# Two feed-forwards on one core: the high and low part of h side by side in one 512-column product

## The chip, the cores and the metric

The kernel runs on one core of one Trainium2 chip, in one launch. The metric is the device time of one execution in microseconds. TensorE multiplies matrices, VectorE and ScalarE do elementwise work, GpSimd a little of it, and SyncE issues most of the transfers.

## The reference, cut to what matters

The whole program is a small model of 256 tokens with width 1024: two blocks with attention mixers and a feed-forward each, then a block with a delta-rule mixer and a layer of product-key experts. Only the two feed-forwards (layers 0 and 1) are touched:

```python
h = rms_norm(x, ffn_norm[i]) * (1.0 + sc_f) + sh_f
x = x + g_f * swiglu(h, ffn_w_gate[i], ffn_w_up[i], ffn_w_down[i])
```

Here `swiglu` is `(silu(h @ w_gate) * (h @ w_up)) @ w_down`, with 2816 hidden columns. All is float32.

## The kernel before

A float32 value is held as a high part, rounded to the format that TensorE multiplies in one pass (fp32r), and a low part, the remainder. A product of two such values is three products: high by high, low by high and high by low. The fourth is left out.

A feed-forward is one stage, `swiglu` (L1625). The 2816 hidden columns are cut into 22 tiles of 128. For tile i the weights are u (gate and up columns, 1 MB, halves 0 and 1 of 1024 columns) and v (down rows, 0.5 MB). The normed and modulated h lies turned, as `h_hi` and `h_lo`, each 128 x 8 x 256. The work of tile i:

- SyncE loads u, v and a chunk of the modulation weights of the next layer (1 MB), on one queue, u and v three tiles ahead.
- ScalarE casts u to its high part (`high_u`, L1773), VectorE subtracts to get the low part (`low_u`, L1809); v the same way (L1779, L1814).
- TensorE, `up(i)`: for each half and each of 8 chunks of the inner dimension three products with 256 columns (the tokens), L1728 to L1730, summed in PSUM tile `pa`. The first tile is in `up_first` (L1713 to L1715), interleaved with the transposes of the norm (L544).
- ScalarE takes Silu of the gate half (L1798), VectorE multiplies it by the up half (L1838), rounds (L1842) and subtracts (L1844): the coefficients `c_hi` and `c_lo`.
- TensorE, `down(i)`: 12 products with 512 columns (L1742, L1743, L1746), summed over all tiles in `py`.

TensorE's order is `up_first`, two products that sum a gate row over the partitions (`Sums`, L221; layer 0 only), and then `up(i)`, `down(i-1)` for i from 1 to 21, and `down(21)`. ScalarE's order per tile is Silu(i), cast of u for tile i+2, cast of v for tile i+1. VectorE's is multiply, round, subtract, low part of u for i+2, low part of v for i+1, and then the modulation's folds: `Modulation.fold` (L200) multiplies a chunk of weights by a column and adds it to a row, 128 x 2048. `fold_at` spreads the folds over tiles 2 to 20; one tile has none, one or two. Layer 0 folds each of 20 chunks into one row. Layer 1 folds its first 8 chunks into two rows and 12 into one. Each engine runs its own list in order; between engines there are semaphores, and each buffer of u_hi, u_lo, v_hi, v_lo, c_hi, c_lo, pa and act_out exists twice. After the last tile the sum in `py` is scaled and added to x (L1860, L1862).

Of the kernel before, what the change touches and what calls it, by code (L numbers as in the profile page):

```python
# [1624 lines left out]
def swiglu(nc, name, k, feeds, h_split, x, ahead, gate, ada, row, feeds_ahead):  # L1625
# [4 lines left out]
    h_hi, h_lo = h_split  # L1630
    first = ada[2]
    chunks = ada[3] - first
    with Stage(nc, name) as st:
        sums = Sums(nc, k, st, row, (10, 11), 2) if row is not None else None
        u_hi, u_lo = (st.sb(n, [P, 2, 2 * D], F32R) for n in ("u_hi", "u_lo"))
        v_hi, v_lo = (st.sb(n, [P, 2, D], F32R) for n in ("v_hi", "v_lo"))
        act_out = st.sb("act_out", [P, 2, S])
        coef = st.sb("coef", [P, S])
        c_hi, c_lo = (st.sb(n, [P, 2, S], F32R) for n in ("c_hi", "c_lo"))
        pa = st.ps("pa", [P, 2, CW])  # L1640
        py = st.ps("py", [P, TT * 2, CW])
# [15 lines left out]
        pcols = pa[:, tiles % 2, 0:2 * KT]  # L1657
# [40 lines left out]
        def _(pe):  # L1698
            def up_first():
# [4 lines left out]
                for c in range(KT):  # L1704
# [3 lines left out]
                    for half in range(2):  # L1708
                        if c % 4 == 0:
                            pe.wait_ge(u_split_first, c // 2 + half + 1)  # L1710
                        out = pa[:, 0, half * S:(half + 1) * S]
                        cols = slice(half * D + c * P, half * D + (c + 1) * P)
                        pe.matmul(out, u_hi[:, 0, cols], h_hi[:, c, :], start=(c == 0 and half == 0), stop=False)  # L1713
                        pe.matmul(out, u_hi[:, 0, cols], h_lo[:, c, :], start=False, stop=False)
                        last = pe.matmul(out, u_lo[:, 0, cols], h_hi[:, c, :], start=False,  # L1715
                                         stop=(c == KT - 1 and half == 1))
# [40 lines left out]
            pe.wait_ge(weighed, tiles - 1)  # L1757
# [48 lines left out]
        def _(dve):  # L1806
# [26 lines left out]
            for i in range(tiles):  # L1833
                b = i % 2
                dve.wait_ge(acted, i + 1)
                if i >= 1:
# [1960 lines left out]
```

## Time and profile before

| | |
|---|---|
| time, median of 3 runs | 2159.97 us (2158.83 to 2162.43) |
| the profiled execution | 2154.51 us, span 2152.7 us |
| granted TensorE clock, mean | 0.955 |
| TensorE busy (matmuls) | 1963.3 us, 91% of the span |
| VectorE busy | 1616.8 us, 75% |
| ScalarE busy | 982.0 us, 46% |
| tiles of layer 0's feed-forward | about 253 to 450 us of the span |
| tiles of layer 1's feed-forward | about 624 to 827 us of the span |

The profile is of one execution. Matmuls are pipelined, so the record of one lasts until its results are out and overlaps the next; their spacing is read from starts. A granted clock of 1.00 is 2.4 GHz, 0.50 is 1.2 GHz. An arrow in a row names the instruction that ended the idle time ahead of it. Starts are microseconds from the start of the span.

### The profile page before, as it was taken

What the parts mean: (1) busy time and instruction counts of PE and PEld (TensorE: products, weight loads), DVE (VectorE), ACT (ScalarE), POOL (GpSimd) and SP (SyncE); (2) the same over time, 40 slices, a digit from 0 to 9 for tenths busy, and PEclk for the clock granted to TensorE, in tenths of its full rate; (3) what the DMA queues carried; (4) which work ended last, traced back from release to release, by engine and by line L of the source; (5) the groups of instructions that cost most, each with busy time, mean ns of one, the idle gap of its engine ahead of it and who ended that gap; (6) DMA issues with size and microseconds to landing.
All of it is one profiled execution on the core that took longest, in us unless ns stands there. A gap on an engine that the chain in (4) does not pass through costs nothing. (4 is left out here: it accounts for less than half of the span.)

```text
span 2152.7 us, 40884 instructions
## 1 busy us (share of the span) xinstructions
PE 1963.3 (91%) x16381; PEld 1775.2 (82%) x16381; DVE 1616.8 (75%) x2682; ACT 982.0 (46%) x1758; POOL 437.4 (20%) x238
## 2 busy tenths in 40 slices
PE   8967899989779998998788888999999999999997
PEld 4954899988579997878787878999999998888886
DVE  3757787857658996776566574599999997877786
ACT  2527434336554333324344544454455554445553
POOL 1000000000230001431000300478677770000000
PEclk9979999989889998997899989999999999999999
DMA  7771698825148792312200034466566666777775
GB/s 251 254 201 60 229 341 310 287 108 193 64 147 292 284 342 89 103 55 81 79 4 4 2 138 157 154 219 206 188 196 200 199 205 216 243 243 240 241 243 192
DMA packets 184769, 390.65 MB, mean 181 GB/s; under 512 B 14922, under 2 KB 130298, under 8 KB 173050
## 3 DMA queue, kind: packets, MB, share of 16 engines
q1 hardware_dynamic: 166050, 371.21, 51.5%
q10 hardware_dynamic: 18530, 16.82, 2.3%
q8 instruction: 131, 2.15, 0.4%
q14 instruction: 58, 0.48, 0.1%
HBM read 368.58 MB, written 19.40 MB: 180 GB/s over the span
## 5 line engine op out<-in xcount | busy, mean ns | idle before, releaser
L3443 POOL TENSOR_TENSOR peer_lo<-peer_u,peer_hi 128x1024 fp32r<-128x1024 f32 x117 | 299.1, 2561 | 108.4 <-ACT peer_hi L3573 108.3
L3620 PE MATMUL route_pa<-all_h_hi,peer_hi 128*128 128x256 f32 x1024 | 291.6, 285 | 8.3 <-POOL peer_lo L3443 6.5
L3621 PE MATMUL route_pa<-all_h_lo,peer_hi 128*128 128x256 f32 x1024 | 290.7, 284 | 0.0
L3622 PE MATMUL route_pa<-all_h_hi,peer_lo 128*128 128x256 f32 x1024 | 290.5, 284 | 0.0
L1466 ACT CAST peer_hi<-peer_u 128x1024 fp32r<-128x1024 f32 x126 | 132.8, 1054 | 174.4 <-PE experts_py L1449 170.2
L3620 PEld LDWEIGHTS route_pa<-all_h_hi,peer_hi 128*128 128x128 f32 x1024 | 197.3, 193 | 9.9 <-POOL peer_lo L3443 7.9
L1445 PE MATMUL experts_py<-peer_hi,experts_c_hi 128*128 128x512 f32 x512 | 200.3, 391 | 3.6 <-DVE experts_c_lo L1506 3.6
L1446 PE MATMUL experts_py<-peer_lo,experts_c_hi 128*128 128x512 f32 x512 | 200.2, 391 | 0.0
L3621 PEld LDWEIGHTS route_pa<-all_h_lo,peer_hi 128*128 128x128 f32 x1024 | 197.3, 193 | 0.0
L3622 PEld LDWEIGHTS route_pa<-all_h_hi,peer_lo 128*128 128x128 f32 x1024 | 197.2, 193 | 0.0
L1728 PE MATMUL ffn_pa<-all_h_hi,ffn_u_hi 128*128 128x256 f32 x672 | 191.2, 285 | 3.0 <-DVE ffn_u_lo L1809 3.0
L1730 PE MATMUL ffn_pa<-all_h_hi,ffn_u_lo 128*128 128x256 f32 x672 | 191.2, 285 | 0.0
L1729 PE MATMUL ffn_pa<-all_h_lo,ffn_u_hi 128*128 128x256 f32 x672 | 191.1, 284 | 0.0
L1449 PE MATMUL experts_py<-peer_hi,experts_c_lo 128*128 128x512 f32 x512 | 158.2, 390 | 0.0
L1500 DVE TENSOR_TENSOR peer_lo<-peer_u,peer_hi 128x1024 fp32r<-128x1024 f32 x126 | 153.5, 1219 | 0.0
L3579 ACT ACTIVATE peer_g<-route_pa 128x256 f32<-128x256 f32 x128 | 49.1, 383 | 195.4 <-PE route_pa L3622 195.4
L3573 ACT CAST peer_hi<-peer_u 128x1024 fp32r<-128x1024 f32 x127 | 133.6, 1052 | 2.7 <-DMA peer_u<-in_peer_u 2.5
L1728 PEld LDWEIGHTS ffn_pa<-all_h_hi,ffn_u_hi 128*128 128x128 f32 x672 | 129.8, 193 | 5.6 <-DVE ffn_u_lo L1809 4.0
L1729 PEld LDWEIGHTS ffn_pa<-all_h_lo,ffn_u_hi 128*128 128x128 f32 x672 | 129.8, 193 | 1.5
L1730 PEld LDWEIGHTS ffn_pa<-all_h_hi,ffn_u_lo 128*128 128x128 f32 x672 | 129.8, 193 | 0.0
L876 PE MATMUL proj_psum<-proj_w_hi,all_h_hi 128*128 128x256 f32 (+1 forms) x384 | 112.2, 292 | 13.0 <-DVE proj_w_lo L912 13.0
L1445 PEld LDWEIGHTS experts_py<-peer_hi,experts_c_hi 128*128 128x128 f32 x512 | 96.4, 188 | 24.3 <-DVE experts_c_lo L1506 3.1
(608 smaller groups left out, 5313.8 us busy)
## 6 DMA issues: line engine op xcount, KB each, us to landing
peer_u<-in_peer_v SPq DMA_DIRECT2D x128, 512.0 KB, 3.8
peer_u<-in_peer_u SPq DMA_DIRECT2D x125, 512.0 KB, 3.6
l_w<-in_ffn_columns SPq DMA_DIRECT2D x44, 1024.0 KB, 8.8
ffn_ada_w<-in_ada_w SPq DMA_DIRECT2D x40, 1024.0 KB, 6.1
ffnw_v<-in_ffn_rows SPq DMA_DIRECT2D x44, 512.0 KB, 4.8
hid_kept<-peer_g ACTq DMA_DIRECT2D x128, 128.0 KB, 1.7
all_main<-hid_kept SPq DMA_DIRECT2D x128, 128.0 KB, 3.7
l_w<-in_diff_w_in SPq DMA_DIRECT2D x12, 1024.0 KB, 5.5
```

Source lines behind the costliest of these rows:

```text
L1445: pe.matmul(py[:, 2 * t + n, :], c_hi[:, b, part], v_hi[:, r, cols], start=start, stop=False)
L1446: pe.matmul(py[:, 2 * t + n, :], c_hi[:, b, part], v_lo[:, r, cols], start=False, stop=False)
L1449: last = pe.matmul(py[:, 2 * t + n, :], c_lo[:, b, part], v_hi[:, r, cols], start=False, stop=stop)
L1500: dve.tensor_tensor(v_lo[:, r, :], feed_v.slot(i), v_hi[:, r, :].bitcast(F32), ALU.subtract).then_inc(v_split, 1)
L1728: pe.matmul(out, u_hi[:, b, cols], h_hi[:, c, :], start=(c == 0), stop=False)
L1729: pe.matmul(out, u_hi[:, b, cols], h_lo[:, c, :], start=False, stop=False)
L1730: last = pe.matmul(out, u_lo[:, b, cols], h_hi[:, c, :], start=False, stop=(c == KT - 1))
L3443: pool.tensor_tensor(u_lo[:, i % ring, :], raw_u(i), u_hi[:, i % ring, :].bitcast(F32), ALU.subtract).then_inc(u_split, 1)
L3573: act.copy(u_hi[:, i % ring, cols], raw_u(i)[:, cols]).then_inc(u_hi_ready, 1)
L3620: pe.matmul(out, u_hi[:, b, cols], h_hi[:, c, :], start=(c == 0), stop=False)
L3621: pe.matmul(out, u_hi[:, b, cols], h_lo[:, c, :], start=False, stop=False)
L3622: last = pe.matmul(out, u_lo[:, b, cols], h_hi[:, c, :], start=False, stop=(c == KT - 1))
```

## The change

`h_hi` and `h_lo` become the two halves of one tile `h_pair`, so that for a chunk their columns lie side by side. The high part of a weight is then multiplied by both with one product of 512 columns, whose two halves of 256 are different sums; the low part of the weight is multiplied by `h_hi` into the first half. `pa` grows to four banks (two tiles by gate and up). ScalarE copies the second halves (gate and up, 2 x 256) out of PSUM to `second`, and VectorE adds them to the first halves: first the gate's, then the up's. Silu then runs on the sum in SBUF. The summing of the gate row uses `pa`'s second half as its PSUM and stands ahead of `up_first`; `up(1)` waits until its results are copied out.

```diff
-    def __init__(self, nc, k, st, row, jobs, banks):
+    def __init__(self, nc, k, st, row, jobs, banks, psum=None):
-        self.psum = st.ps("sum_psum", [P, banks, CW])
+        self.psum = st.ps("sum_psum", [P, banks, CW]) if psum is None else psum
...
-        act_out = st.sb("act_out", [P, 2, S])
-        coef = st.sb("coef", [P, S])
+        gate_sum, up_sum = (st.sb(n, [P, 2, S]) for n in ("gate_sum", "up_sum"))
-        pa = st.ps("pa", [P, 2, CW])
+        pa = st.ps("pa", [P, 2, 2, CW])
+        sums = Sums(nc, k, st, row, (10, 11), 2, pa[:, 1]) if row is not None else None
...
+        second = full[:, 0:2, :]
...
+            def row_products(pe, b, half, c):
+                cols = slice(half * D + c * P, half * D + (c + 1) * P)
+                pe.matmul(pa[:, b, half, :], u_hi[:, b, cols], h_pair[:, c].rearrange("p a s -> p (a s)"),
+                          start=(c == 0), stop=False)
+                return pe.matmul(pa[:, b, half, 0:S], u_lo[:, b, cols], h_hi[:, c, :], start=False, stop=(c == KT - 1))
...
             def up(i):
...
                 if i >= 2:
-                    pe.wait_ge(weighed, i - 1)
+                    pe.wait_ge(up_summed, i - 1)
+                elif sums:
+                    pe.wait_ge(sums.moved, len(sums.jobs))
                 for half in range(2):
-                    out = pa[:, b, half * S:(half + 1) * S]
                     for c in range(KT):
-                        cols = slice(half * D + c * P, half * D + (c + 1) * P)
-                        pe.matmul(out, u_hi[:, b, cols], h_hi[:, c, :], start=(c == 0), stop=False)
-                        pe.matmul(out, u_hi[:, b, cols], h_lo[:, c, :], start=False, stop=False)
-                        last = pe.matmul(out, u_lo[:, b, cols], h_hi[:, c, :], start=False, stop=(c == KT - 1))
+                        last = row_products(pe, b, half, c)
...
-            up_first()
             if sums:
                 sums.sum(pe)
+            up_first()
...
                 act.wait_ge(rows_ready, i + 1)
-                if i >= 2:
-                    act.wait_ge(weighed, i - 1)
-                act.activation(act_out[:, i % 2, :], pa[:, i % 2, 0:S], ACT.Silu).then_inc(acted, 1)
+                if i:
+                    act.wait_ge(up_summed, i)
+                act.copy(second, pa[:, i % 2, :, S:2 * S]).then_inc(second_ready, 1)
+                act.wait_ge(gate_summed, i + 1)
+                act.activation(gate_sum[:, i % 2, :], gate_sum[:, i % 2, :], ACT.Silu).then_inc(acted, 1)
...
+                dve.wait_ge(second_ready, i + 1)
+                if i >= 2:
+                    dve.wait_ge(coef_ready, i - 1)
+                for half, (to, done) in enumerate(((gate_sum, gate_summed), (up_sum, up_summed))):
+                    dve.tensor_tensor(to[:, b, :], pa[:, b, half, 0:S], second[:, half, :], ALU.add).then_inc(done, 1)
+                dve.wait_ge(up_summed, i + 1)
                 dve.wait_ge(acted, i + 1)
-                if i >= 1:
-                    dve.wait_ge(coef_ready, i)
-                dve.tensor_tensor(coef[:], act_out[:, b, :], pa[:, b, S:2 * S], ALU.mult).then_inc(weighed, 1)
+                dve.tensor_tensor(up_sum[:, b, :], gate_sum[:, b, :], up_sum[:, b, :], ALU.mult).then_inc(weighed, 1)
...
-                dve.tensor_copy(c_hi[:, b, :], coef[:]).then_inc(rounded, 1)
+                dve.tensor_copy(c_hi[:, b, :], up_sum[:, b, :]).then_inc(rounded, 1)
...
-        h_hi, h_lo = (pst.sb(n, [P, KT, S], F32R) for n in ("h_hi", "h_lo"))
-        k["h_hi"], k["h_lo"] = h_hi, h_lo
+        k["h_pair"] = pst.sb("h_pair", [P, KT, 2, S], F32R)
+        k["h_hi"], k["h_lo"] = (k["h_pair"][:, :, i, :] for i in range(2))
```

## Rows read from the trace of the kernel before

**Rows 1.** The page's first part: busy time, share of the span, instructions.

```profile
PE 1963.3 (91%) x16381; PEld 1775.2 (82%) x16381; DVE 1616.8 (75%) x2682; ACT 982.0 (46%) x1758; POOL 437.4 (20%) x238
```

**Rows 2.** Busy time by stretch, tiles of layer 0 and 1; clock, DMA share and GB/s last.

```profile
267.00:447.00 180.00, 180.00 (x1264) 169.32 (x1263) 139.83 (x127) 68.07 (x65) 0.67 (x1) 1.00 0.84 295
647.00:825.00 178.00, 177.75 (x1251) 167.16 (x1250) 155.36 (x135) 63.81 (x61) 0.00 (x0) 1.00 0.78 281
```

**Rows 3.** TensorE's timeline in one tile of layer 0: start, us, instruction.

```profile
299.80 0.28 PE L1728 MATMUL ffn_pa<-all_h_hi,ffn_u_hi 128*128 128x256 f32 x1
...
305.56 0.40 PE L1742 MATMUL ffn_py<-ffn_v_hi,ffn_c_hi 128*128 128x512 f32 x1
...
308.30 0.28 PE L1728 MATMUL ffn_pa<-all_h_hi,ffn_u_hi 128*128 128x256 f32 x1
```

**Rows 4.** Groups of instructions, 645 to 825 us (layer 1): busy, mean ns, idle before.

```profile
L200 DVE SCALAR_TENSOR_TENSOR all_main<-ffn_ada_w,all_main 128x2048 f32<-128x2048 f32 x28 | 65.4, 2347 | 0.5
...
L1809 DVE TENSOR_TENSOR ffn_u_lo<-l_w,ffn_u_hi 128x2048 fp32r<-128x2048 f32 x19 | 43.5, 2288 | 6.1 <-ACT ffn_u_hi L1773 6.1
...
L1838 DVE TENSOR_TENSOR ffn_coef<-ffn_act_out,ffn_pa 128x256 f32<-128x256 f32 x21 | 8.8, 418 | 10.5 <-ACT ffn_act_out L1798 10.5
```

**Rows 5.** ScalarE and VectorE, timeline of one tile of layer 0.

```profile
305.75 0.38 ACT L1798 ACTIVATE ffn_act_out<-ffn_pa 128x256 f32<-128x256 f32 x1 [4.64 <-PE ffn_pa L1730]
...
306.04 1.91 ACT L1773 CAST ffn_u_hi<-l_w 128x2048 fp32r<-128x2048 f32 x1
306.17 0.42 DVE L1838 TENSOR_TENSOR ffn_coef<-ffn_act_out,ffn_pa 128x256 f32<-128x256 f32 x1 [0.95 <-ACT ffn_act_out L1798]
...
306.63 0.29 DVE L1842 CAST ffn_c_hi<-ffn_coef 128x256 fp32r<-128x256 f32 x1
...
306.96 0.42 DVE L1844 TENSOR_TENSOR ffn_c_lo<-ffn_coef,ffn_c_hi 128x256 fp32r<-128x256 f32 x1
...
307.98 2.29 DVE L1809 TENSOR_TENSOR ffn_u_lo<-l_w,ffn_u_hi 128x2048 fp32r<-128x2048 f32 x1 [0.60 <-ACT ffn_u_hi L1773]
...
310.19 1.22 DVE L1814 TENSOR_TENSOR ffn_v_lo<-ffnw_v,ffn_v_hi 128x1024 fp32r<-128x1024 f32 x1
...
311.32 2.35 DVE L200 SCALAR_TENSOR_TENSOR all_main<-ffn_ada_w,all_main 128x2048 f32<-128x2048 f32 x1
```

**Rows 6.** VectorE's timeline in layer 1: two folds in one tile, and the multiply behind.

```profile
676.92 4.80 DVE L200 SCALAR_TENSOR_TENSOR all_main<-ffn_ada_w,all_main 128x2048 f32<-128x2048 f32 x2
681.64 0.41 DVE L1838 TENSOR_TENSOR ffn_coef<-ffn_act_out,ffn_pa 128x256 f32<-128x256 f32 x1
...
693.92 4.61 DVE L200 SCALAR_TENSOR_TENSOR all_main<-ffn_ada_w,all_main 128x2048 f32<-128x2048 f32 x2
698.45 0.41 DVE L1838 TENSOR_TENSOR ffn_coef<-ffn_act_out,ffn_pa 128x256 f32<-128x256 f32 x1
```

**Rows 7.** Groups of ScalarE: the copy of 128x512 out of PSUM.

```profile
L227 ACT COPY all_main<-ffn_sum_psum 128x512 f32<-128x512 f32 x2 | 1.2, 585 | 0.3 <-PE ffn_sum_psum L221 0.3
```

**Rows 8.** Both stages' heads: timeline of TensorE, second Silu, and busy time by stretch.

```profile
250.95 1.86 PE L544 MATMUL ffn_py<-ffn_norm_diag,all_main 128*128 128x128 f32 x7 [3.41 <-DVE ffn_norm_diag L568]
...
263.19 1.88 PE L221 MATMUL ffn_sum_psum<-all_main,all_ones 128*128 128x512 f32 x4
265.70 0.39 PE L1728 MATMUL ffn_pa<-all_h_hi,ffn_u_hi 128*128 128x256 f32 x1 [0.63 <-DVE ffn_u_lo L1809]
...
271.75 0.39 ACT L1798 ACTIVATE ffn_act_out<-ffn_pa 128x256 f32<-128x256 f32 x1 [1.62 <-PE ffn_pa L1730]
...
638.30 0.39 PE L1728 MATMUL ffn_pa<-all_h_hi,ffn_u_hi 128*128 128x256 f32 x1 [2.35 <-DVE ffn_u_lo L1809]
...
645.86 0.38 ACT L1798 ACTIVATE ffn_act_out<-ffn_pa 128x256 f32<-128x256 f32 x1 [4.56 <-PE ffn_pa L1730]
...
250.00:256.00 6.00, 5.05 (x23) 5.02 (x24) 4.75 (x13) 3.10 (x6) 0.00 (x0) 0.50 0.56 225
638.00:642.00 4.00, 3.70 (x18) 3.71 (x19) 3.93 (x6) 3.28 (x4) 4.00 (x3) 0.59 0.38 121
```

More of the change, by code:

```diff
@@ L1630, in swiglu @@
     h_hi, h_lo = h_split
+    h_pair = k["h_pair"]
     first = ada[2]
@@ L1633, in swiglu @@
     with Stage(nc, name) as st:
-        sums = Sums(nc, k, st, row, (10, 11), 2) if row is not None else None
         u_hi, u_lo = (st.sb(n, [P, 2, 2 * D], F32R) for n in ("u_hi", "u_lo"))
         v_hi, v_lo = (st.sb(n, [P, 2, D], F32R) for n in ("v_hi", "v_lo"))
-        act_out = st.sb("act_out", [P, 2, S])
-        coef = st.sb("coef", [P, S])
+        gate_sum, up_sum = (st.sb(n, [P, 2, S]) for n in ("gate_sum", "up_sum"))
         c_hi, c_lo = (st.sb(n, [P, 2, S], F32R) for n in ("c_hi", "c_lo"))
-        pa = st.ps("pa", [P, 2, CW])
+        pa = st.ps("pa", [P, 2, 2, CW])
         py = st.ps("py", [P, TT * 2, CW])
-        u_hi_ready, u_split, v_hi_ready, v_split, rows_ready, acted, weighed, rounded, coef_ready, down_done, \
+        sums = Sums(nc, k, st, row, (10, 11), 2, pa[:, 1]) if row is not None else None
+        u_hi_ready, u_split, v_hi_ready, v_split, rows_ready, second_ready, gate_summed, up_summed, acted, weighed, rounded, coef_ready, down_done, \
             scaled, summed = (st.sem(n) for n in (
-                "u_hi_ready", "u_split", "v_hi_ready", "v_split", "rows_ready", "acted", "weighed", "rounded",
-                "coef_ready", "down_done", "scaled", "added"))
+                "u_hi_ready", "u_split", "v_hi_ready", "v_split", "rows_ready", "second_ready", "gate_summed",
+                "up_summed", "acted", "weighed", "rounded", "coef_ready", "down_done", "scaled", "added"))
         beside = Modulation(nc, k, st, *ada)
@@ L1656, in swiglu @@
         columns = Columns(st, k, "ahead", *ahead, k["cols"])
-        pcols = pa[:, tiles % 2, 0:2 * KT]
+        pcols = pa[:, tiles % 2, 0, 0:2 * KT]
         tmp = feed_v.slot(0).rearrange("p (a n) -> p a n", a=2)
@@ L1710, in up_first @@
                             pe.wait_ge(u_split_first, c // 2 + half + 1)
-                        out = pa[:, 0, half * S:(half + 1) * S]
-                        cols = slice(half * D + c * P, half * D + (c + 1) * P)
[L1713 to L1716, printed above, removed]
+                        last = row_products(pe, 0, half, c)
                 last.then_inc(rows_ready, 1)
@@ L1722, in up @@
                 if i >= 2:
-                    pe.wait_ge(weighed, i - 1)
+                    pe.wait_ge(up_summed, i - 1)
+                elif sums:
+                    pe.wait_ge(sums.moved, len(sums.jobs))
                 for half in range(2):
-                    out = pa[:, b, half * S:(half + 1) * S]
                     for c in range(KT):
-                        cols = slice(half * D + c * P, half * D + (c + 1) * P)
-                        pe.matmul(out, u_hi[:, b, cols], h_hi[:, c, :], start=(c == 0), stop=False)
-                        pe.matmul(out, u_hi[:, b, cols], h_lo[:, c, :], start=False, stop=False)
-                        last = pe.matmul(out, u_lo[:, b, cols], h_hi[:, c, :], start=False, stop=(c == KT - 1))
+                        last = row_products(pe, b, half, c)
                 last.then_inc(rows_ready, 1)
@@ L1756, in _ @@
             down(tiles - 1)
-            pe.wait_ge(weighed, tiles - 1)
+            pe.wait_ge(up_summed, tiles - 1)
             pe.wait_ge(beside.folded, chunks)
@@ L1841, in _ @@
                     dve.wait_ge(down_done, i - 1)
-                dve.tensor_copy(c_hi[:, b, :], coef[:]).then_inc(rounded, 1)
+                dve.tensor_copy(c_hi[:, b, :], up_sum[:, b, :]).then_inc(rounded, 1)
                 dve.wait_ge(rounded, i + 1)
-                dve.tensor_tensor(c_lo[:, b, :], coef[:], c_hi[:, b, :].bitcast(F32), ALU.subtract
+                dve.tensor_tensor(c_lo[:, b, :], up_sum[:, b, :], c_hi[:, b, :].bitcast(F32), ALU.subtract
                                   ).then_inc(coef_ready, 1)
```

## The prediction, made before the change was timed

> **What bounds the kernel now.** I read the page's first part, then the busy time by stretch, then the timeline inside one feed-forward tile, because the change touches nothing outside the two feed-forward stages. Over the whole span TensorE is busy 91% and VectorE 75% [rows 1], but both are averages over many stages. In the two stretches that hold nearly all of the feed-forward tiles TensorE is busy 180.00 of 180.00 us and 177.75 of 178.00 us at a granted clock of 1.00, VectorE 139.83 of 180.00 in layer 0 and 155.36 of 178.00 in layer 1 [rows 2]. So TensorE bounds both stages, and in layer 1 VectorE is only 13% behind it.
>
> Matmul records overlap, so their durations (0.28 us for 256 columns, 0.40 us for 512, [rows 3]) are no price; the distance between starts is. In one tile of layer 0 the 48 products with 256 columns take 299.80 to 305.56, 5.76 us or 120.0 ns each; the 12 products with 512 columns take 305.56 to 308.30, 2.74 us or 228.3 ns each [rows 3]. The two together are a tile: 8.50 us.
>
> VectorE's tile comes from starts in the same way [rows 5]: gate multiply 306.17, rounding 306.63, remainder 306.96, then nothing until 307.98, because the low part of u waits for ScalarE's cast of u (306.04 + 1.91 = 307.95); low part of u 2.21 us to the next start, low part of v 1.13 us, then the modulation folds. Two folds in a row take 4.72 us (676.92 to 681.64) or 4.53 us (693.92 to 698.45) [rows 6]; I take 2.31 us for one. Layer 0 has 20 folds for tiles 2 to 20. Layer 1 has 28, because its first 8 chunks are folded into two rows [rows 4].
>
> **TensorE's part.** Each (chunk, half) had three 256-column products, 3 x 120.0 = 360 ns; it now has one of 512 and one of 256, 228.3 + 120.0 = 348 ns. The columns streamed are the same 768. 16 pairs per tile save 0.19 us: a tile of 8.31 us. For 21 tiles of a stage after the first that is 3.9 us. In the first tile the products run between the norm's transposes, and its 16 pairs save 0.2 us. The trace has no 512 followed by a 256 with other weights; the bounds are 0 (360 ns) and 40 ns (768 columns at the 2.4 GHz that a granted clock of 1.00 is, 320 ns). I take 12, by the rows of the same stage.
>
> The row on this first: 120.0 ns for 256 columns and 228.3 for 512 leave about 13 to 15 ns per matmul above the columns' own time. The Trainium skill, TensorE: Matmul & The Clock Gate, section Back-to-back issue gap, gives for isolated matmuls columns / 2.4 GHz plus about 2.5 ns; by that rule one matmul less would be worth 2.5 ns, not 12. The trace does not agree with it in size, so the rows decide; what a small saving would do is a rival below.
>
> **VectorE's part.** Added per tile: two additions of 128x256, one operand in PSUM. The nearest row is today's gate multiply with the same shape and operands, 418 ns [rows 4]. The multiply, now all in SBUF, I leave at its price. Removed: nothing. The additions are 0.84 us per tile of busy time.
>
> **ScalarE's part.** Added: one copy of 128x512 out of PSUM, 585 ns [rows 7]. ScalarE is busy 68.07 of 180.00 us [rows 2], so the copy itself is covered. It costs through its place: Silu and the cast of u stand behind it and behind the new wait for VectorE's gate sum. Today, when VectorE is late, ScalarE has run ahead, its cast is done, and VectorE does not wait: over all of layer 1 the low part of u waited only 6.1 us for it [rows 4], though one wait is 0.60 us [rows 5] and there are 20 tiles. After the change Silu(i) needs the gate sum of tile i, and the cast of u for tile i+2 is queued behind Silu(i). So VectorE waits for that cast in every tile, however late it is itself.
>
> VectorE's tile from the start of the gate addition, all steps from [rows 5]: addition 0.42, to ScalarE 0.04 (305.75 + 0.38 to 306.17, the other way round), Silu's start to cast's start 0.29 (305.75 to 306.04), cast and handover 1.94. The low part of u starts at 2.69. Inside this lie the second addition, the multiply (from 0.88), rounding (1.34) and remainder (1.67, done at 2.09): they leave VectorE idle for 0.6. Then 2.21 + 1.13: folds start at 6.03.
>
> *Layer 0:* tiles 2 to 20 take 19 x 6.03 + 20 x 2.31 = 160.8 us, less 2.9 in tile 20, which has no u left to split (its low part of v starts at 2.0 and not at 4.90): 157.9. TensorE needs 19 x 8.31 = 157.9. A tie: TensorE keeps its gain, with no reserve. At the end the last coefficient comes at 0.82 (handover, copy 0.59, handover) + 2.14 = 2.96 us after the last u product, while the down product of the tile before covers 2.74: 0.2 us exposed. Sum: -3.9 - 0.2 + 0.2 = -3.9.
>
> *Layer 1:* 19 x 6.03 + 28 x 2.31 - 2.9 = 176.4 us. TensorE needs 157.9. **VectorE becomes the bound.** Buffers let it lag some 5 us, but this lag is not forgiven at the end, since the last down product needs the last coefficient. From the end of tile 2's u products to the end of the last down product: 0.82 + 176.4 + 2.14 + 2.74 = 182.1. Today: 19 x 8.50 + 2 x 2.74 = 167.0. So +15.1, less 0.6 that the tiles 0 to 2 save on TensorE: +14.5.
>
> **The moved sums (layer 0 only).** Two products of the gate row stood between the first tile and the second at 263.19 [rows 8], taking 1.9 us in time in which TensorE would have waited for the low part of u anyway: it still idled 0.63 us until 265.70 [rows 8]. They now run at the stage's start, before the transposes, where TensorE is idle for 3.41 us until 250.95 [rows 8]. They come ahead of the transposes on the queue; at full clock they are covered, at half clock (3.8 us) they delay them by about 0.7. ScalarE's moves of their results (two of 585 ns, [rows 7]) stand behind the first cast of v and end before 265.7, so the second tile waits for nothing new. Two sides through the clock: today the head, 250 to 256, runs at a granted 0.50, which is 1.2 GHz, after that idle stretch [rows 8]. 5.05 us were busy there; if the sums keep the clock up, at most 2.5 come back; I take 2.0. The gap they filled is left empty, as it is in layer 1 today: 2.35 us idle before 638.30, and then 0.59 granted in 638 to 642 [rows 8]. From the second tile's first product to its Silu it takes 7.56 us there (638.30 to 645.86), against 6.05 in layer 0 (265.70 to 271.75) [rows 8]: 1.5 lost. Net -0.5, with bounds -2.0 and +2.2.
>
> The one layout change, h_hi and h_lo as halves of one tile, leaves each slice contiguous; I cost it at nothing for every other stage.
>
> **Sum.** -3.9 (layer 0) + 14.5 (layer 1) - 0.5 (sums) = +10.1 us. The profiled execution took 2154.51 us (span 2152.7), so the same execution would give 2164.6; the median of the three runs is 5.5 higher, 2159.97, and from it I get **2170 us**, 0.5% slower.
>
> **The rivals.** What the measurement can tell from no change is 0.2%, 4.3 us.
> 1. *VectorE keeps TensorE's pace in layer 1* (the other side). It decides from a VectorE tile of 8.31 us, that is 4.9 without the folds' 3.4 (28 x 2.31 / 19), where I have 6.03. Then both layers keep TensorE's gain: twice -4.1 (21 x 0.19 and 0.2 at the head) less 0.2 each at the end, -0.5 for the sums: -8.3, 2152. For it: VectorE idles 22.6 us in layer 1 now [rows 2], more than 19 x 0.84 = 16 us of additions. Against it: the wait for the cast must vanish and the additions shrink by half. Chance 0.09.
> 2. *Only the wait for the cast vanishes.* VectorE's steps back to back are 0.34 + 0.46 + 0.46 + 0.33 + 0.34 + 2.21 + 1.13 = 5.27 us; layer 1 then takes 19 x 0.76 - 0.8 = 13.7 us less than forecast (in tile 20 nothing waited for a cast): -3.6, 2156 to 2160 with the bounds, mostly within 0.2%. Against it: the program order on ScalarE. Chance 0.09. That matmul records mean what they say (3 x 0.28 against 0.40 + 0.28 us, 704 pairs, 113 us less) is excluded by the starts 120 ns apart.
> 3. *The smaller saving.* With 0 to 3 ns per pair layer 0 gains nothing and layer 1 does not change: +14.5, 2174. By the rule cited above it would be 352 x 2.5 ns = 0.9 us in layer 0, 2173. Chance 0.2, inside the forecast's range.
> 4. *The clock falls in the waits of layer 1.* TensorE would idle about 1 us per tile, up to 2.3 in one piece behind two folds, as long as the gap before 638.30. Each fall costs about 1.5 us, but the idle time takes it in while VectorE is the bound. 0 to +4: 2174. Chance 0.12.
> The forecast with rivals 3 and 4: 0.82.
>
> **How the numbers follow.** Layer 1 between +12 (folds at 2.26, quicker handovers) and +19 (clock, slower ones); layer 0 between -4.5, VectorE's tie, and +0.5; sums -2.0 to +2.2. Likely together +2.5 to +18.5: 2162.5 to 2178.5. That leaves out rivals 1 and 2 and little else, under 0.2.
>
> **What would show it.** Right: in layer 1 starts of Silu (now every 8.50 us) 9.3 apart on average, TensorE waiting there some 15 us for coefficients or the low part of u; VectorE's low part of u waiting about 0.6 us for ScalarE's cast in nearly each tile of both layers; in layer 0 a period of 8.31 and the 512-column product followed 228 ns later. Wrong: TensorE still busy all of layer 1's stretch; additions under 0.3 us; pairs at 360 ns or 330; a VectorE that starts the low part of u right behind the remainder.

## The result, and the profile after

The changed kernel takes 2172.33 us (median of 9 runs, 2167.78 to 2177.0) against 2159.97 (9 runs, 2155.27 to 2165.2): a ratio of 1.0059 (1.0044 to 1.0075), 0.6% slower. The forecast was 2170, range 2162.5 to 2178.5.

The page's first part, of the changed kernel, answers to [rows 1]:

```profile
span 2171.5 us, 39659 instructions
...
PE 1968.2 (91%) x15677; PEld 1740.3 (80%) x15677; DVE 1648.2 (76%) x2770; ACT 1006.1 (46%) x1802; POOL 437.5 (20%) x238
```

704 matmuls fewer, 88 VectorE and 44 ScalarE instructions more. The span of this one execution is 18.8 us longer than that of the one before, where the medians differ by 12.4. Of the 18.8, 14.8 lie in the two stages, and the rest, 1.4 ahead of them and 2.6 behind, in code that did not change.

Each stage begins with ScalarE's Square (L549), so the distance to the next stage's Square is the stage's time. Instructions of line L549, kernel before; the last two numbers of a row are the first and last start:

```profile
L549 ACT ACTIVATE ffn_full<-all_main x2: 1057/1057/1057, 248.1 to 621.2; 128x1024 f32<-128x1024 f32 x2
...
L549 ACT ACTIVATE proj_full<-all_main x1: 1057/1057/1057, 453.1 to 453.1; 128x1024 f32<-128x1024 f32 x1
...
L549 ACT ACTIVATE dnb_h_t<-all_main x1: 1057/1057/1057, 827.2 to 827.2; 128x1024 f32<-128x1024 f32 x1
```

The same of the changed kernel:

```profile
L549 ACT ACTIVATE ffn_full<-all_main x2: 1057/1057/1057, 249.5 to 621.5; 128x1024 f32<-128x1024 f32 x2
...
L549 ACT ACTIVATE proj_full<-all_main x1: 1057/1057/1057, 453.5 to 453.5; 128x1024 f32<-128x1024 f32 x1
...
L549 ACT ACTIVATE dnb_h_t<-all_main x1: 1057/1057/1057, 843.3 to 843.3; 128x1024 f32<-128x1024 f32 x1
```

Layer 0: 205.0 before, 204.0 after, -1.0. Layer 1: 206.0 before, 221.8 after, **+15.8**. Between the two stages, all of the loss is in layer 1. These two differences are of one execution of each kernel; runs below whose code in a stage is the same as here differ there by 1.3 us (layer 1) and 2.1 us (layer 0).

What the span gained behind the two stages is in large part one place, 32 products of one column each (L509) in the delta-rule mixer. TensorE's timeline, kernel before and changed kernel:

```profile
1259.98 3.77 PE L509 MATMUL dnon_pcols<-all_ones,all_main 128*128 128x1 f32 x32
...
1276.32 6.83 PE L509 MATMUL dnon_pcols<-all_ones,all_main 128*128 128x1 f32 x32
```

The granted clock is 1.00 in the first (1260.0 to 1263.0 us) and 0.50 in the second (1276.3 to 1279.3): 3.1 us for the same instructions. In the profiles of all eleven kernels with the new feed-forward (this one and e1 to e3, e5 to e11) they take 6.8 us, in those of the kernel before and e4 3.8. So this seems to come with the change, though by what path no run shows.

Busy time by stretch of the changed kernel (the first two answer to [rows 2], the last two to the heads in [rows 8]; clock, DMA share and GB/s last):

```profile
267.00:447.00 180.00, 179.84 (x931) 152.91 (x931) 154.62 (x170) 78.80 (x86) 0.30 (x1) 0.99 0.84 295
647.00:825.00 178.00, 168.33 (x848) 140.64 (x847) 159.78 (x160) 69.96 (x77) 0.00 (x0) 0.97 0.79 277
...
250.00:256.00 6.00, 4.59 (x25) 3.20 (x24) 4.86 (x14) 4.44 (x11) 0.00 (x0) 1.00 0.74 264
266.00:272.00 6.00, 6.00 (x22) 5.13 (x21) 5.20 (x8) 3.81 (x4) 1.30 (x1) 0.55 0.64 199
```

TensorE still fills layer 0 and no longer fills layer 1, where it idles 9.7 of 178 us. VectorE's groups in layer 1 (645 to 840 us; busy, mean ns, idle before) answer to [rows 4]:

```profile
L200 DVE SCALAR_TENSOR_TENSOR all_main<-ffn_ada_w,all_main 128x2048 f32<-128x2048 f32 x28 | 65.4, 2346 | 0.5
L1811 DVE TENSOR_TENSOR ffn_u_lo<-l_w,ffn_u_hi 128x2048 fp32r<-128x2048 f32 x20 | 45.8, 2292 | 9.8 <-ACT ffn_u_hi L1773 9.8
...
L1844 DVE TENSOR_TENSOR ffn_up_sum<-ffn_gate_sum,ffn_up_sum 128x256 f32<-128x256 f32 x21 | 8.9, 426 | 4.7 <-ACT ffn_gate_sum L1800 4.7
...
L1841 DVE TENSOR_TENSOR ffn_gate_sum<-ffn_pa,ffn_full 128x256 f32<-128x256 f32 x21 | 8.8, 417 | 2.7 <-ACT ffn_full L1798 2.7
L1841 DVE TENSOR_TENSOR ffn_up_sum<-ffn_pa,ffn_full 128x256 f32<-128x256 f32 x21 | 8.7, 414 | 0.0
```

The additions cost 415 ns each, as priced. VectorE waits for its input (L1841) only 2.7 us in 21 tiles: it is the bound. TensorE in turn waits for VectorE's coefficients:

```profile
PE ffn_py L1742 <- DVE ffn_c_lo L1850: 10.5, 8, 2.1
```

(From `--waits`, 640 to 838 us: us in total, times, longest.) The prediction had some 15 us here. And yet VectorE waits 9.8 + 4.7 us for ScalarE inside its own chain. One tile of layer 0 in VectorE's timeline shows how, beside [rows 5]:

```profile
318.70 0.42 DVE L1841 TENSOR_TENSOR ffn_gate_sum<-ffn_pa,ffn_full 128x256 f32<-128x256 f32 x1
319.03 0.41 DVE L1841 TENSOR_TENSOR ffn_up_sum<-ffn_pa,ffn_full 128x256 f32<-128x256 f32 x1
319.67 0.43 DVE L1844 TENSOR_TENSOR ffn_up_sum<-ffn_gate_sum,ffn_up_sum 128x256 f32<-128x256 f32 x1 [0.23 <-ACT ffn_gate_sum L1800]
...
321.40 2.29 DVE L1811 TENSOR_TENSOR ffn_u_lo<-l_w,ffn_u_hi 128x2048 fp32r<-128x2048 f32 x1 [0.52 <-ACT ffn_u_hi L1773]
...
324.75 2.35 DVE L200 SCALAR_TENSOR_TENSOR all_main<-ffn_ada_w,all_main 128x2048 f32<-128x2048 f32 x1
327.01 0.42 DVE L1841 TENSOR_TENSOR ffn_gate_sum<-ffn_pa,ffn_full 128x256 f32<-128x256 f32 x1
```

The low part of u starts 2.70 us behind the gate addition (forecast 2.69), the fold 6.05 (forecast 6.03), the next tile 8.31. In layer 1 the gate additions of tiles 2 and 21 start at 655.53 and 831.86, 176.3 us apart (9.28 us a tile); the forecast was 176.4.

TensorE's timeline in a tile of layer 0 of the changed kernel, against [rows 3]:

```profile
302.75 0.40 PE L1702 MATMUL ffn_pa<-all_h_pair,ffn_u_hi 128*128 128x512 f32 x1
302.98 0.28 PE L1704 MATMUL ffn_pa<-all_h_pair,ffn_u_lo 128*128 128x256 f32 x1
303.09 0.40 PE L1702 MATMUL ffn_pa<-all_h_pair,ffn_u_hi 128*128 128x512 f32 x1
303.33 0.28 PE L1704 MATMUL ffn_pa<-all_h_pair,ffn_u_lo 128*128 128x256 f32 x1
303.44 0.40 PE L1702 MATMUL ffn_pa<-all_h_pair,ffn_u_hi 128*128 128x512 f32 x1
```

Over the 16 pairs from 301.69 to 307.33 a pair takes 352.5 ns: 239 behind the wide product and 114 behind the narrow one. It saves 7.5 ns, not 12, and TensorE's tile is 8.385 us, not 8.31.

### The profile page after: what moved, and what is told of

The parts are those of the page before. It is cut to its first block and busy times, and to the rows that moved or that the text cites. A ratio compares the mean times of both kernels' runs of the same rounds, so it can differ in the third digit from the quotient of the medians.

```text
span 2171.5 us, 39659 instructions
## 1 busy us (share of the span) xinstructions
PE 1968.2 (91%) x15677; PEld 1740.3 (80%) x15677; DVE 1648.2 (76%) x2770; ACT 1006.1 (46%) x1802; POOL 437.5 (20%) x238
## 5 line engine op out<-in xcount | busy, mean ns | idle before, releaser
L3626 PE MATMUL route_pa<-all_h_pair,peer_hi 128*128 128x256 f32 x1024 | 291.9, 285 | 7.5 <-POOL peer_lo L3449 5.7
L3627 PE MATMUL route_pa<-all_h_pair,peer_hi 128*128 128x256 f32 x1024 | 291.1, 284 | 0.0
L3628 PE MATMUL route_pa<-all_h_pair,peer_lo 128*128 128x256 f32 x1024 | 291.0, 284 | 0.0
L1702 PE MATMUL ffn_pa<-all_h_pair,ffn_u_hi 128*128 128x512 f32 x704 | 257.0, 406 | 5.4 <-DVE ffn_u_lo L1811 4.7
L3626 PEld LDWEIGHTS route_pa<-all_h_pair,peer_hi 128*128 128x128 f32 x1024 | 197.8, 193 | 9.0 <-POOL peer_lo L3449 6.9
L1704 PE MATMUL ffn_pa<-all_h_pair,ffn_u_lo 128*128 128x256 f32 x704 | 199.6, 284 | 0.0
L3628 PEld LDWEIGHTS route_pa<-all_h_pair,peer_lo 128*128 128x128 f32 x1024 | 197.8, 193 | 0.0
L3627 PEld LDWEIGHTS route_pa<-all_h_pair,peer_hi 128*128 128x128 f32 x1024 | 197.8, 193 | 0.0
L1702 PEld LDWEIGHTS ffn_pa<-all_h_pair,ffn_u_hi 128*128 128x128 f32 x704 | 135.0, 192 | 40.0 <-DVE ffn_u_lo L1811 6.3
L1704 PEld LDWEIGHTS ffn_pa<-all_h_pair,ffn_u_lo 128*128 128x128 f32 x704 | 135.5, 193 | 1.4
L876 PE MATMUL proj_psum<-proj_w_hi,all_h_pair 128*128 128x256 f32 (+1 forms) x384 | 112.2, 292 | 13.2 <-DVE proj_w_lo L912 13.2
L200 DVE SCALAR_TENSOR_TENSOR all_main<-ffn_ada_w,all_main 128x2048 f32<-128x2048 f32 x48 | 112.3, 2346 | 0.6
```

The costliest lines, as they stand in the source:

```text
L1702: pe.matmul(pa[:, b, half, :], u_hi[:, b, cols], h_pair[:, c].rearrange("p a s -> p (a s)"), start=(c == 0), stop=False)
L1704: return pe.matmul(pa[:, b, half, 0:S], u_lo[:, b, cols], h_hi[:, c, :], start=False, stop=(c == KT - 1))
```

## The experiments

Two theories of the result: (A) VectorE's tile bounds layer 1, through the additions and, nearly as much, through the waits that ScalarE's and VectorE's orders impose on each other; (B) the additions alone, or TensorE itself, are slower and the waits cost nothing. Stage times are distances between L549's starts, as above.

**e1: folds between the additions and the multiply.**

```diff
                     dve.tensor_tensor(to[:, b, :], pa[:, b, half, 0:S], second[:, half, :], ALU.add).then_inc(done, 1)
+                for n, fold in enumerate(folds):
+                    if fold_at[n] == i:
+                        beside.fold(dve, *fold)
...
-                for n, fold in enumerate(folds):
-                    if fold_at[n] == i:
-                        beside.fold(dve, *fold)
```

> The changed kernel with VectorE's folds put between its two additions and the multiply; no work added or left out. Theory (VectorE's tile bounds layer 1, and 0.22 + 0.52 us of it are waits for ScalarE's Silu and cast that its own order makes): both waits vanish in tiles with a fold, the low part of u starts right behind the remainder, VectorE's tile is 5.2 + folds, layer 1's stage (221.8 us from its first Square to the next stage's) falls to about 207.5, layer 0 stays at 204, the whole is about 14 us below the changed kernel, near the kernel before. Rival (only the two additions, 0.84 us a tile, slow VectorE; the waits are only where it would have stood idle anyway): layer 1 stays within 3 us of 221.8.

Measured: 2198.65 us, ratio to the kernel before 1.0196 (1.0177 to 1.0216); layer 0 takes 211.5, layer 1 239.2. A miss, in the wrong direction. VectorE's groups in e1, first layer 1 and then layer 0:

```profile
L200 DVE SCALAR_TENSOR_TENSOR all_main<-ffn_ada_w,all_main 128x2048 f32<-128x2048 f32 x28 | 65.4, 2347 | 31.8 <-DMA ffn_ada_w<-in_ada_w 31.6
L1811 DVE TENSOR_TENSOR ffn_u_lo<-l_w,ffn_u_hi 128x2048 fp32r<-128x2048 f32 x21 | 48.0, 2285 | 1.6 <-ACT ffn_u_hi L1773 1.6
...
L200 DVE SCALAR_TENSOR_TENSOR all_main<-ffn_ada_w,all_main 128x2048 f32<-128x2048 f32 x20 | 46.9, 2344 | 8.5 <-DMA ffn_ada_w<-in_ada_w 8.4
```

The waits for ScalarE did go (1.6 us for the cast where it was 9.8). In their place came waits for the modulation weights, 31.6 and 8.4 us. SyncE asks for a chunk in a turn of its loop that waits for the low parts of u and v of an earlier tile, late in VectorE's order, and a tile's first fold now stands right behind the additions, not 6.05 us behind the gate addition: it needs its weights some 5 us sooner. So this run says nothing yet on A against B, only that the fold's place and SyncE's order belong together; e9 moves both.

**e3 and e4: layer 1 with 20 folds in place of 28**, in the changed kernel and in the kernel before. Both leave out work that the program needs.

```diff
-        folds = [(chunk, v) for chunk in range(first, ada[3]) for v in range(len(beside.rows(chunk)))]
+        folds = [(chunk, len(beside.rows(chunk)) - 1) for chunk in range(first, ada[3])]
```

> The changed kernel without the 8 folds of layer 1 into the second row (the modulation of the context is left out). Theory (VectorE bound): layer 1's stage loses 8 x 2.31 = 18.5 us until TensorE binds at 8.385 a tile, so it falls from 221.8 to about 204. Rival (TensorE is slowed itself, by its clock in short waits or by the pairs): layer 1 hardly moves, at most 4 us.

> The kernel before without the same 8 folds. Theory: TensorE bounds layer 1 there, so its stage stays at 206.0 within 0.5 us and the whole within the noise of the kernel before. Rival (VectorE was already part of the bound in layer 1): 2 us or more less.

Measured: e3 2151.79 us, ratio to the kernel before 0.9981 (0.9968 to 0.9995), layer 1 falls from 221.8 to 203.5. e4 2157.18 us, 0.9996 (0.9982 to 1.0009), layer 1 at 205.9. Eight folds are 18.3 us in the changed kernel and nothing in the one before: VectorE bounds layer 1 after the change and did not before it. With TensorE as the bound again (8.39 us a tile), layer 1 takes 203.5, 2.5 below the kernel before.

e3's layer 0 has the same instructions in the same order as the changed kernel's, and takes 201.9 us (248.7 to 450.6) where that took 204.0. This is taken up under e6.

**e5: the pairs alone.**

```diff
-                act.copy(second, pa[:, i % 2, :, S:2 * S]).then_inc(second_ready, 1)
-                act.wait_ge(gate_summed, i + 1)
-                act.activation(gate_sum[:, i % 2, :], gate_sum[:, i % 2, :], ACT.Silu).then_inc(acted, 1)
+                act.activation(gate_sum[:, i % 2, :], pa[:, i % 2, 0, 0:S], ACT.Silu).then_inc(acted, 1)
...
-                for half, (to, done) in enumerate(((gate_sum, gate_summed), (up_sum, up_summed))):
-                    dve.tensor_tensor(to[:, b, :], pa[:, b, half, 0:S], second[:, half, :], ALU.add).then_inc(done, 1)
...
-                dve.tensor_tensor(up_sum[:, b, :], gate_sum[:, b, :], up_sum[:, b, :], ALU.mult).then_inc(weighed, 1)
+                dve.tensor_tensor(up_sum[:, b, :], gate_sum[:, b, :], pa[:, b, 1, 0:S], ALU.mult).then_inc(weighed, 1)
```

> The changed kernel's products alone: the second halves are neither copied nor added (the term with the low part of h is left out), Silu and multiply read PSUM as in the kernel before. Shows what the pairs are worth where TensorE binds. Theory from the trace of the changed kernel (352.5 ns a pair against 360): tile of 8.385 us, 42 x 0.115 = 4.8 us less than the kernel before, and 0.9 us more at the head of layer 0; about 4 us below the kernel before. By the prediction's 348 ns: 8 us. By the Trainium skill's 2.5 ns a matmul: below 2 us.

Measured: 2151.98 us, 0.9967 (0.9953 to 0.998), 5.6 us or 0.33% less; layer 0 takes 201.3, layer 1 202.9. Silus in layer 1, ScalarE's timeline of e5:

```profile
701.17 0.38 ACT L1798 ACTIVATE ffn_gate_sum<-ffn_pa 128x256 f32<-128x256 f32 x1 [4.53 <-PE ffn_pa L1704]
709.55 0.39 ACT L1798 ACTIVATE ffn_gate_sum<-ffn_pa 128x256 f32<-128x256 f32 x1 [4.53 <-PE ffn_pa L1704]
717.94 0.39 ACT L1798 ACTIVATE ffn_gate_sum<-ffn_pa 128x256 f32<-128x256 f32 x1 [4.54 <-PE ffn_pa L1704]
```

A period of 8.385 us against 8.50: this is all that the wide product itself gives in a tile, and the additions must not cost more than that. The period agrees with the trace's 7.5 ns a pair, and neither with 12 nor with 2.5. The whole time doesn't separate the first two: its interval is 4.3 to 10.1 us less, and the 8 us of the 12 ns lie in it.

**e2: the low part of v on GpSimd.**

```diff
+            for i in range(tiles):
+                pool.wait_ge(v_hi_ready, i + 1)
+                pool.tensor_tensor(v_lo[:, i % 2, :], feed_v.slot(i), v_hi[:, i % 2, :].bitcast(F32), ALU.subtract
+                                   ).then_inc(v_split, 1)
...
-                if i + 1 < tiles:
-                    low_v(i + 1)
```

> The changed kernel with the low part of v made by GpSimd and not by VectorE. Theory: VectorE's tile is 1.13 shorter, 4.92 + folds, on average 8.32 in layer 1 against TensorE's 8.385; layer 1's stage falls from 221.8 to about 206. If the two engines hold each other up (in the kernel before a rounding of 0.29 took 0.67 us while GpSimd's memset ran), VectorE's tile grows again by 0.4 or more, and layer 1 stays at 210 or above.

Measured: 2216.4 us, 1.028 (1.0259 to 1.03); layer 0 takes 222.5, layer 1 245.1. A clear miss. VectorE's and GpSimd's timelines of e2, in one tile of layer 0:

```profile
325.32 2.29 DVE L1815 TENSOR_TENSOR ffn_u_lo<-l_w,ffn_u_hi 128x2048 fp32r<-128x2048 f32 x1 [0.51 <-ACT ffn_u_hi L1777]
327.53 4.49 DVE L200 SCALAR_TENSOR_TENSOR all_main<-ffn_ada_w,all_main 128x2048 f32<-128x2048 f32 x1
...
326.32 3.55 POOL L1699 TENSOR_TENSOR ffn_v_lo<-ffnw_v,ffn_v_hi 128x1024 fp32r<-128x1024 f32 x1 [5.76 <-ACT ffn_v_hi L1783]
```

The fold takes 4.49 us in place of 2.35. It ends 2.15 us behind the end of GpSimd's subtraction (329.87), less than a fold takes by itself, as if it had stood still until GpSimd was done. GpSimd's subtraction, issued while the low part of u ran, takes 3.55 us, where the fastest of this run takes 2.37; from the end of the low part of u (327.61) it is 2.26. VectorE gave away 1.13 us and lost 2.14. What the trace shows is that two such instructions don't run beside each other. The Trainium skill, SBUF — State Buffer, section Who interferes with whom, says that a VectorE instruction with two SBUF inputs contends with a GpSimd instruction that reads SBUF, over a shared read interface; it calls the shared ports an exclusive lock and says that the order of issue decides who blocks. The trace agrees: the later one waited in both cases.

**e7 and e8: e1 and e2 together**, e8 with the gate row's products behind the first tile.

> The changed kernel with the folds between additions and multiply and the low part of v on GpSimd. Theory: VectorE's tile is 4.0 + folds, 7.4 on average in layer 1, so TensorE binds both layers at 8.385 a tile: layer 1 about 203.5, 4 us below the kernel before in all. If the port is shared, VectorE has 1 us to spare and nothing changes.

> The same with the gate row's products behind the first tile again. Theory: 1 us less than with them ahead, some 5 us (0.2%) below the kernel before.

Measured: e7 2196.48 us (1.0176, 1.0151 to 1.0201), e8 2193.16 (1.017, 1.0149 to 1.0191). In e7 layer 0 takes 210.8 and layer 1 235.8, in e8 209.7 and 235.3. Both carry the faults of e1 and e2, so the spare microsecond did not help: in e7's layer 1 the multiply, now beside GpSimd's subtraction, takes 1424 ns on average in place of 426, and the folds still wait 9.2 us for weights. They tell little beyond e1 and e2.

**e6: the gate row's products back behind the first tile.**

```diff
+            up_first()
             if sums:
                 sums.sum(pe)
-            up_first()
```

> The changed kernel with the two products of the gate row back behind the first tile. Theory: the clock trade is undone. The head of layer 0 runs at a granted 0.50 again and its last transposed chunk is placed 1.7 us later, the gap behind the first tile is filled, so the second tile's products take 5.7 instead of 8.6 us: together 0.9 to 1.2 us less, layer 0's stage 203 instead of 204. Rival (the place does nothing): 204.0, and granted clocks as in the changed kernel.

Measured: 2170.85 us, 1.0062 (1.0039 to 1.0085), which the noise of the whole can't tell from the changed kernel. In the profiled execution layer 0 takes 202.7 against 204.0. Busy time by stretch of e6, clock third from the end:

```profile
250.00:256.00 6.00, 3.67 (x15) 3.54 (x16) 4.39 (x12) 4.49 (x10) 0.00 (x0) 0.53 0.78 264
...
266.00:272.00 6.00, 5.23 (x30) 4.55 (x30) 4.86 (x8) 5.53 (x6) 2.75 (x2) 1.00 0.44 140
```

Beside the rows of the changed kernel this looks like the trade that was expected: with the products ahead the head at a granted 1.00 (2.4 GHz) and the second tile at 0.55 (mostly 1.2 GHz), with them behind 0.53 and 1.00. But e3 has the products ahead and layer 0's instructions unchanged, and its execution shows another course. Busy time by stretch of e3, then TensorE's and ScalarE's timelines, the second tile's first product and the copy of its sums:

```profile
250.00:256.00 6.00, 5.55 (x25) 3.85 (x24) 4.36 (x14) 4.03 (x9) 0.00 (x0) 0.72 0.67 253
266.00:272.00 6.00, 6.00 (x34) 5.15 (x33) 5.19 (x8) 4.19 (x5) 1.08 (x1) 1.00 0.76 226
...
265.11 0.50 PE L1702 MATMUL ffn_pa<-all_h_pair,ffn_u_hi 128*128 128x512 f32 x1 [2.36 <-DVE ffn_u_lo L1811]
...
271.06 0.59 ACT L1798 COPY ffn_full<-ffn_pa 128x512 f32<-128x512 f32 x1 [1.34 <-PE ffn_pa L1704]
```

TensorE sat idle 2.36 us in the gap ahead of the second tile, where it was 2.37 in the changed kernel's execution, but here the clock did not fall: the second tile takes 5.95 us from its first product to ScalarE's copy, where it took 8.6 there, and layer 0 takes 201.9, less than e6's 202.7. In e1, with the same order at the head, the tile takes 7.2 (264.65 to 271.86). So where the clock falls differs between executions with the same instructions in the head, and one profile on each side doesn't price the move of the products: these give anything from 1.3 us dearer to 0.8 us cheaper than e6. What the fall itself costs can be read: 2.6 us between 5.95 and 8.6.

e6's layer 1, whose code is that of the changed kernel, takes 220.5 against 221.8, for a like reason: in the stage's first 12 us the granted clock is 0.76 (620.1 to 632.1) where it was 0.65 (621.5 to 633.5), and the gate addition of tile 2 starts 32.7 us into the stage where it was 34.0. From there to tile 21 both take 176.3.

**e9 and e10: the folds between, with their weights asked for sooner; and wide and narrow products grouped.** Both with e6's order of the sums.

```diff
-        load_at = [ring if c < 2 else done_at[c - 2] + 4 for c in range(chunks)]
+        load_at = [ring if c < 2 else done_at[c - 2] + 3 for c in range(chunks)]
```

> Folds between additions and multiply as in e1, but each chunk of modulation weights is asked for one turn of SyncE's loop sooner, and the gate row's products stand behind the first tile. Theory (e1 lost its time only to folds that waited for their weights: 31.6 us in layer 1 and 8.4 in layer 0; ScalarE's hold on VectorE costs 0.74 us a tile): those waits go below 3 us in all, VectorE's tile is 5.2 + folds = 8.55 on average, layer 1's stage falls from 221.8 to 206 to 209, layer 0's is 202.7 as in e6, and the whole is within 3 us of the kernel before, 12 below the changed one. Rival (the hold costs nothing, the additions everything): layer 1 at 219 or more even with the weights there.

In e10 also:

```diff
-                for half in range(2):
-                    for c in range(KT):
-                        last = row_products(pe, b, half, c)
+                for c in range(KT):
+                    for half in range(2):
...
+                        pe.matmul(pa[:, b, half, :], u_hi[:, b, cols], h_pair[:, c].rearrange("p a s -> p (a s)"),
+                                  start=(c == 0), stop=False)
+                    for half in range(2):
...
+                        last = pe.matmul(pa[:, b, half, 0:S], u_lo[:, b, cols], h_hi[:, c, :], start=False,
+                                         stop=(c == KT - 1))
```

> The same as e9, with the two 512-column products of a chunk (gate, up) in a row and then the two of 256 columns, so that wide and narrow ones change half as often. Theory (the 239 ns behind a wide product against 228 among its like come from the change to a narrow one): a mean of 350 ns or less a pair, layer 0's period 8.35 or below where it was 8.385. Rival (it comes from something else, or from PSUM banks): the same or longer.

Measured: e9 2156.53 us, 1.0 (0.999 to 1.0009); layer 0 202.8, layer 1 **205.7** in place of 221.8. VectorE's groups of e9, layer 1:

```profile
L200 DVE SCALAR_TENSOR_TENSOR all_main<-ffn_ada_w,all_main 128x2048 f32<-128x2048 f32 x28 | 65.3, 2345 | 0.6 <-DMA ffn_ada_w<-in_ada_w 0.2
L1811 DVE TENSOR_TENSOR ffn_u_lo<-l_w,ffn_u_hi 128x2048 fp32r<-128x2048 f32 x21 | 48.0, 2286 | 1.5 <-ACT ffn_u_hi L1773 1.5
...
L1847 DVE TENSOR_TENSOR ffn_up_sum<-ffn_gate_sum,ffn_up_sum 128x256 f32<-128x256 f32 x22 | 9.2, 420 | 0.7 <-ACT ffn_gate_sum L1800 0.7
```

No work is left out, the additions are all there, and layer 1 is 16.1 us shorter. Between the gate additions of tiles 2 and 21 it was 176.3 us and is 161.6 (653.27 to 814.82), 14.8 less. In the timeline between these two the waits for Silu and the cast were 4.2 + 9.3 = 13.5 us and are gone; new ones are 1.9 for tile 21's copy and 0.2 for weights; the other 3.4 are steps that follow each other more closely with no wait between them. The remaining 1.3 lies ahead of tile 2; e6 gained the same there with layer 1 unchanged, so it is not the order's. Theory A holds in its second half as well; theory B, 219 or more, is out.

e10 2156.05 us, 0.9988 (0.9974 to 1.0002). TensorE's timeline of e10, layer 0:

```profile
326.50 0.62 PE L1731 MATMUL ffn_pa<-all_h_pair,ffn_u_hi 128*128 128x512 f32 x2
326.95 0.40 PE L1735 MATMUL ffn_pa<-all_h_pair,ffn_u_lo 128*128 128x256 f32 x2
327.18 0.63 PE L1731 MATMUL ffn_pa<-all_h_pair,ffn_u_hi 128*128 128x512 f32 x2
327.65 0.39 PE L1735 MATMUL ffn_pa<-all_h_pair,ffn_u_lo 128*128 128x256 f32 x2
```

Over 8 groups two pairs take 0.465 + 0.230 = 0.695 us, 347.5 ns a pair, and the period in layer 0 is 8.29 us. That is the forecast's 348: the price was right for products among their like, and the alternation of wide and narrow costs 5 ns a pair. Layer 0 takes 200.9; layer 1, where VectorE still bounds with 8.52 a tile on average (654.07 to 815.87 for 19), stays at 205.9.

**e11: the rounding on ScalarE.** e10, and:

```diff
+                act.wait_ge(weighed, i + 1)
+                if i >= 2:
+                    act.wait_ge(down_done, i - 1)
+                act.copy(c_hi[:, i % 2, :], up_sum[:, i % 2, :]).then_inc(rounded, 1)
...
-                dve.wait_ge(weighed, i + 1)
-                if i >= 2:
-                    dve.wait_ge(down_done, i - 1)
-                dve.tensor_copy(c_hi[:, b, :], up_sum[:, b, :]).then_inc(rounded, 1)
+                if i + 1 < tiles:
+                    low_v(i + 1)
                 dve.wait_ge(rounded, i + 1)
```

> e10 with the rounding of the coefficients (c_hi) moved from VectorE to ScalarE, behind its cast of v, and VectorE's low part of v put between multiply and remainder. Theory (in e10 VectorE, 8.55 us a tile, still bounds layer 1 and TensorE, 8.29 a tile, layer 0): VectorE's tile is 4.7 + folds, 8.1 on average, TensorE binds both layers, layer 1's stage falls from 205.9 to about 201.5, layer 0's stays at 200.9, and the whole is 7 to 9 us (0.3 to 0.4%) below the kernel before. Rival (the handovers to ScalarE and back come too late for the down product behind two folds): layer 1 at 205 or more.

Measured: 2151.06 us beside 2154.64 for the kernel before on that chip, ratio 0.998 (0.9967 to 0.9994); layer 0 202.4, layer 1 202.2. Groups of e11, 645 to 822 us, TensorE's and VectorE's:

```profile
L1748 PE MATMUL ffn_py<-ffn_v_hi,ffn_c_hi 128*128 128x512 f32 x85 | 33.6, 395 | 0.3 <-DVE ffn_c_lo L1861 0.3
...
L1861 DVE TENSOR_TENSOR ffn_c_lo<-ffn_up_sum,ffn_c_hi 128x256 fp32r<-128x256 f32 x21 | 8.8, 420 | 0.5 <-ACT ffn_c_hi L1814 0.5
```

TensorE waits 0.3 us for coefficients in all of layer 1: it is the bound again. This version is faster than both kernels, by 0.2% against the one before (an interval that only just leaves out no difference), less than the 0.3 to 0.4% expected. By its profile the two stages are 2.6 + 3.8 = 6.4 us shorter than before, where 4.1 + 4.5 were expected, and the whole only 3.6; the L509 products in the delta-rule mixer take 3.1 us more, as in the changed kernel, which is about the gap. Layer 0 takes 1.5 us more than e10's 200.9. Timeline of e11, VectorE and TensorE, around the first tile's coefficients:

```profile
270.97 1.23 DVE L1826 TENSOR_TENSOR ffn_v_lo<-ffnw_v,ffn_v_hi 128x1024 fp32r<-128x1024 f32 x1 [2.25 <-ACT ffn_v_hi L1785]
272.12 0.42 DVE L1861 TENSOR_TENSOR ffn_c_lo<-ffn_up_sum,ffn_c_hi 128x256 fp32r<-128x256 f32 x1
...
272.59 0.50 PE L1748 MATMUL ffn_py<-ffn_v_hi,ffn_c_hi 128*128 128x512 f32 x1 [0.66 <-DVE ffn_c_lo L1861]
```

In the first tiles, which have no fold, the low part of v now stands ahead of the remainder and waits 2.25 us for ScalarE's cast; the coefficients come late, and TensorE waits. ScalarE's copies of tiles 1 and 2 are 9.25 us apart there (271.96 to 281.21), where later ones are 8.29: about 1 of the 1.5 us. The rest was not separated, and is less than two executions of the same code differed by above.

## Why the prediction was right

- *Layer 1 becomes VectorE's.* Right in kind and size: +14.5 forecast, +15.8 measured (+14.5 in e6, whose layer 1 is the same code), the chain from tile 2 to tile 21 176.4 against 176.3 us. The step that carried it was the order on ScalarE (Silu and the cast of u behind VectorE's gate sum). The waits in a tile are 0.52 us for the cast and 0.22 for Silu, where the sum had 0.6 idle in all. e3, e4 and e9 show it by taking away the load, then the waits.
- *The pairs.* Direction right, size off: 7.5 ns a pair where the sum took 12, so 2.4 us per stage where it took 3.9 (between tiles 2 and 21 of layer 0 159.3 us against 161.5 before). That step failed: it took a 512-column product's price from twelve in sequence, as [rows 3] have them; e10 gives 348 back when like follows like. In layer 0 this is 1.5 us, in layer 1 nothing.
- *The sums.* Both effects are seen, but the order alone does not fix either, as the forecast had it. In the changed kernel's profiled execution the head gave 1.7 us back (2.0 forecast), and the second tile took 8.6 us from its first product to ScalarE's read (265.33 to 273.97), where 6.05 is the row of before: 2.6 lost, not 1.5; net +0.9 and not -0.5. In e3's execution of the same code the head gave 1.2, the second tile lost nothing, and the sign is the other way. What decides between the two courses stays open. Both lie within the forecast's bounds of -2.0 and +2.2.
- *Layer 0.* -3.9 - 0.5 = -4.4 forecast; -1.0 measured, and -3.1 in e3. Of the 3.4 us between forecast and profile 1.5 are the pairs and 1.4 the sums; 0.5 was not separated. The tie between VectorE (8.31) and TensorE (8.385) came out much as forecast: TensorE binds, with VectorE 0.07 below it.
- *Tiles 0 to 2 of layer 1* were to give 0.6. The copy of tile 2 starts 33.4 us into the stage where Silu did at 33.2, so that here 0.2 is lost; in e6 it starts at 32.05, 1.1 less. The clock in the stage's head makes the difference, as e6 shows.
- *The sum*: +10.1 forecast, +12.4 measured in the medians. The profiled executions show +14.8 in the two stages, 3.4 of the difference in layer 0 and 1.3 in layer 1. With e3's layer 0 and e6's layer 1, the same code in other executions, it would be +11.4. Two terms were wrong in every execution: the pairs' 12 ns, and the nothing that was put down for all other stages, where the L509 products took 3.1 us more. That the median came out only 2.3 us from the forecast is in part luck. The stated range was also not what its terms add up to: the bounds of layer 1, layer 0 and the sums give +5.5 to +21.7, where the prediction wrote +2.5 to +18.5. The measured +12.4 lies in both.
- *Rivals.* Rival 1 (VectorE keeps pace) and rival 2 (the wait for the cast vanishes) are both things that had to be built. e9 is rival 2: priced at -4 to 0 us against the kernel before, it came out at the upper end (ratio 1.0, 0.9 less in the medians). e11 has rival 1's bound, TensorE in both layers, but not its time: 3.6 us below the kernel before where rival 1 had 8.3; the two stages give 6.4, and what lies outside them takes 2.8 back. Rival 3's smaller saving was half true, and could only be seen in layer 0. Rival 4: TensorE's clock averaged 0.97 in layer 1 (647 to 825 us), but its idle time took that in: the chain was 176.3 us all the same.

## What to carry to other kernels

When an engine is close to being the bound, price a change by that engine's chain through one turn of the loop, with the waits that the other engines' program order forces on it, and not by the busy time it adds: here 0.83 us of additions made a tile, its folds aside, 1.6 us longer (6.05 us from gate sum to fold, where the five instructions of [rows 5], with the wait left out, come to about 4.5). A wait on an engine that used to run ahead is removed by putting independent work (here the folds) between the request and the use, but a moved step takes its transfers' due times with it. Saving an instruction whose columns are streamed anyway was worth only its gap, 7 to 12 ns here. And a stage's time in one profile is not yet the price of a change of 1 or 2 us: look for another run in which that stage is unchanged, and look at the stages that the change does not touch.

## What was not expected of the hardware

- A 512-column product followed by a 256-column one with other weights is 239 ns from it and not 228, the 256 then 114 and not 120. In groups of two like products it is 232 and 115.
- GpSimd's subtraction of 128x1024 and VectorE's folds or multiplies don't run at the same time: 4.49 us for a fold of 2.35, 3.55 for a subtraction whose fastest in the same run takes 2.37.
- The same instructions ran at different granted clocks in different executions: behind an idle gap of 2.37 us the second tile of layer 0 ran at a granted 0.55 in one (266 to 272 us), behind 2.36 us at 1.00 in another (e3).
